# Attention of a hybrid encoder layer: filling projections in side-by-side 64-row products, and the first value products of a pair two key blocks at a time

## The reference

```
gates = sigmoid(gate_logit + gate_b);  g_A, g_B = split(gates)
m = g_A * (y_A @ w_up_gdn) + g_B * (y_B @ w_up_fox)
x = x + m @ w_out;  out = rmsnorm(x)
```

## Time and profile before

| | us |
|---|---|
| median of 3 runs | 946.38 (946.35 to 946.46) |
| the profiled execution itself | 946.32 |
| its span, first to last instruction | 944.5 |
| TensorE busy | 924.9 (98%) |
| VectorE busy | 610.3 (65%) |
| ScalarE busy | 473.1 (50%) |
| granted TensorE clock, mean | 0.999 |

### The profile page before, as it was taken

The page is one execution under the profiler, slowest core; times in us unless marked ns, Lnnn a source line. Parts: engine busy times, 40 slices in busy tenths (PEclk is TensorE's granted clock), DMA queues, the critical chain, the costliest instruction groups (busy, mean ns, idle before and its releaser), DMA issues.

```text
span 944.5 us, 15969 instructions
## 1 busy us (share of the span) xinstructions
PE 924.9 (98%) x6404; PEld 702.3 (74%) x6404; DVE 610.3 (65%) x983; ACT 473.1 (50%) x846; POOL 19.9 (2%) x29
## 2 busy tenths in 40 slices
PE   5999999999999999999999999999999999999997
PEld 5778787888888876676766666666667888888886
DVE  6487668799999934464496786767863433246252
ACT  7555654632866625532756547556554442334132
POOL 1000002020000000000000000000000000000000
PEclk9999999999999999999999999999999999999999
DMA  7111351249323393322553325234125323123162
GB/s 249 47 49 45 98 177 48 69 145 229 96 90 106 107 272 87 102 75 90 139 182 98 105 101 168 102 101 123 34 69 178 113 66 90 55 112 112 41 192 79
DMA packets 114704, 104.87 MB, mean 111 GB/s; under 512 B 33152, under 2 KB 94720, under 8 KB 114248
## 3 DMA queue, kind: packets, MB, share of 16 engines
q1 hardware_dynamic: 103256, 81.05, 30.4%
q10 hardware_dynamic: 10224, 18.62, 5.3%
q0 software_dynamic: 1152, 4.19, 1.4%
HBM read 76.84 MB, written 27.00 MB: 110 GB/s over the span
## 4 chain that ended last, share of the span: by engine, by line
PE 45%; DVE 3%; ACT 1%; DMA 1%; issue 1%; SPq 0%; DVEq 0%; ACTq 0%
PE pj L2287 6%; PE pj L2289 5%; PE pj L2288 5%; PE pc L2420 4%; PE pa L2386 3%; PE pa L2355 1%; PE pj L2298 1%; PE pj L2299 1%; PE pj L2300 1%; PE pj L2558 1%; PE pj L2556 1%; PE pj L2557 1%; PE pb L2446 1%; PE pb L2435 1%; PE pb L2557 1%; PE pb L2556 1%
## 5 line engine op out<-in xcount | busy, mean ns | idle before, releaser
L145 PE MATMUL pj<-h_hi,w_hi 128*128 128x512 f32 x504 | 203.6, 404 | 0.5 <-DVE w_lo L133 0.5
L146 PE MATMUL pj<-h_lo,w_hi 128*128 128x512 f32 x504 | 196.9, 391 | 0.0
L147 PE MATMUL pj<-h_hi,w_lo 128*128 128x512 f32 x504 | 196.5, 390 | 0.0
L145 PEld LDWEIGHTS pj<-h_hi,w_hi 128*128 128x128 f32 x504 | 94.5, 188 | 23.9 <-issue 1.1
L147 PEld LDWEIGHTS pj<-h_hi,w_lo 128*128 128x128 f32 x504 | 94.6, 188 | 20.4
L146 PEld LDWEIGHTS pj<-h_lo,w_hi 128*128 128x128 f32 x504 | 94.7, 188 | 17.9 <-issue 0.2
L2287 PE MATMUL pj<-h_hi,w_hi 128*128 128x512 f32 x248 | 101.3, 408 | 0.3 <-PEq L323 0.3
L2289 PE MATMUL pj<-h_hi,w_lo 128*128 128x512 f32 x248 | 96.8, 390 | 0.0
L2288 PE MATMUL pj<-h_lo,w_hi 128*128 128x512 f32 x248 | 96.7, 390 | 0.0
L2287 PEld LDWEIGHTS pj<-h_hi,w_hi 128*128 128x128 f32 x248 | 46.5, 188 | 19.5 <-issue 10.1
L598 ACT ACTIVATE xc<-pj 128x512 f32<-128x512 f32 x39 | 23.3, 597 | 72.2 <-PE pj L147 71.6
(11 more groups left out here) (372 smaller groups left out, 1867.9 us busy)
## 6 DMA issues: line engine op xcount, KB each, us to landing
w_raw<-in_w_in SPq DMA_DIRECT2D x48, 512.0 KB, 4.4
fox_scratch<-xc ACTq DMA_DIRECT2D x39, 256.0 KB, 2.8
qkv<-in_x SPq DMA_DIRECT2D x8, 512.0 KB, 6.4
fa<-rows_scratch POOLq DMA_DIRECT2D x8, 512.0 KB, 4.9
rv<-fr_scratch SPq DMA_DIRECT2D x16, 256.0 KB, 4.0
ma<-m_scratch SPq DMA_DIRECT2D x8, 512.0 KB, 3.9
rv<-in_w_out SPq DMA_DIRECT2D x8, 512.0 KB, 3.6
w_raw<-in_x SPq DMA_DIRECT2D x8, 512.0 KB, 4.4
```

What stands on the lines that cost most here:

```text
L145: nc.tensor.matmul(o, w_hi[:, slot, k], h_hi[:, k, cols], start=(k == 0), stop=False)
L146: nc.tensor.matmul(o, w_hi[:, slot, k], h_lo[:, k, cols], start=False, stop=False)
L147: last = nc.tensor.matmul(o, w_lo[:, slot, k], h_hi[:, k, cols], start=False, stop=(k == KT - 1))
```

## The change

Fills of tiles 1 to 7 (except one gate half) become groups of 4 k-tiles. A group multiplies the upper 64 rows of a weight with one token half and the lower 64 rows with the other half, side by side, into both halves of `pj`; a second phase swaps the halves, so that after both phases each half has all 128 rows. The number of products in a row is the same: 12 pairs stand in place of 12 whole products. A gate tile takes four groups, an up tile two. Gate and up of a tile now use the same two halves of `pj`, one after the other: an up group waits for both exponentials of the gate, the next gate for both `gated` of the tile. There are 10 groups in a pair, at steps 0, 0, 1, 2, 3, 4, 6, 8, 10, 12.

`exp_a`, `plus`, `sigmoid` and `gated` of both halves follow each other at the same step; there is a second `gate` and `mst` buffer. `gated` moves up in VectorE's steps. `values` of slots 0 and 1 are both issued in slot 2, those of 2 and 3 both ahead of slot 4's `key_scores`. The side buffer for up tile 1 goes; tile 1 is loaded where tile 2 was, its low part is made in step 0 of the first pair.

The schedule:

```diff
+        GROUPS = 10
+        GROUP_STEP = (0, 0, 1, 2, 3, 4, 6, 8, 10, 12)
+        GATE_END = [None, 1] + [7 + 6 * t for t in range(KT - 2)]
+        UP_END = [None, 3] + [9 + 6 * t for t in range(KT - 2)]
...
+        def step_of(group):
+            return -1 if group is None else PER * (group // GROUPS) + GROUP_STEP[group % GROUPS]
```

SyncE:

```diff
                 load_up(0)
-                load_up(1)
                 norm_rows(0)
                 load_raw(2)
                 sp.wait_ge(f_normed, 2)
                 load_v(0)
                 load_fox(fz, 3, 0, fz_loaded)
-                load_up(2)
+                load_up(1)
...
-                        load_up(t + 3)
+                        load_up(t + 2)
```

ScalarE:

```diff
                 def split_up_hi(tile):
+                    act.wait_ge(up_loaded, 32 * tile + 32)
+                    if 1 <= tile <= KT:
+                        act.wait_ge(up_done, 2 * tile)
...
                 def gate_exp(v, psum, dst):
-                    act.wait_ge(pj_done, 2 * N3 + v + 1)
+                    act.wait_ge(pj_done, 2 * N3 + (2 * (v // 2) + 2 if 4 <= v < 2 * KT else v + 1))
...
-                split_up_hi(1)
...
                 exp_a(2)
+                split_up_hi(1)
                 store_m(1)
```

VectorE, `gated`:

```diff
-                    dve.wait_ge(up_done, v + 1)
+                    dve.wait_ge(up_done, 2 * (v // 2) + 2 if v >= 2 else v + 1)
```

VectorE, its loop over the steps:

```diff
                     if s == 0 and p:
                         add_weights(p - 1, SLOTS - 1)
+                        gated_steps(g)
...
                         row_max(p, 0)
                         if p == 0:
-                            gated(1, gate_b1, mst_b1)
+                            gated(1)
+                            split_up_lo(1)
                         row_max(p, 1)
                         row_max(p, 2)
                         row_max(p, 3)
                         low_part(p, 1)
-                        gated_steps(g)
                         spread_max(p, 0)
                         plus_steps(g)
                         gate_steps(g)
                     elif v < 4:
                         if v < 2:
                             row_max(p, 4 + 2 * v)
+                        if v > 1:
+                            add_weights(p, v - 1)
+                        gated_steps(g)
                         if v < 3:
                             plus_steps(g)
-                        if v > 1:
-                            add_weights(p, v - 1)
                         row_max(p, 5 + 2 * v)
```

TensorE, the fills:

```diff
+                def both_halves(w, src, k, phase, first, last, done_sem, turns):
+                    for m, (w_part, s_part) in enumerate(((w[0], src[0]), (w[0], src[1]), (w[1], src[0]))):
+                        for r in range(2):
+                            half = r ^ phase
+                            ins = nc.tensor.matmul(pj[:, half], w_part[half_rows(r)], s_part[half_rows(r), k, half_cols(half)],
+                                                   start=(first and m == 0), stop=(last and m == 2))
...
+                def gate_group(tile, c):
+                    slot = (N3 + tile) % 2
+                    if c == 0:
+                        pe.wait_ge(w_ready, N3 + tile + 1)
+                        pe.wait_ge(up_free, 2 * tile)
+                    phase = c // 2
+                    if c == 2:
+                        pe.wait_ge(phase_done, 4 * tile - 4)
+                    for k in range(4 * (c % 2), 4 * (c % 2) + 4):
+                        both_halves((w_hi[:, slot, k], w_lo[:, slot, k]), (h_hi, h_lo), k, phase,
+                                    phase == 0 and k == 0, phase == 1 and k == KT - 1, pj_done, phase == 0 and k == KT - 1)
...
+                def up_group(tile, phase):
+                    if phase == 0:
+                        pe.wait_ge(up_ready, tile + 1)
+                        pe.wait_ge(pj_free, 2 * N3 + 2 * tile + 4)
...
+                    if n < 2:
+                        for k in range(4 * n, 4 * n + 4):
+                            gate_product(3, k)
```

TensorE, the pair's loop:

```diff
-                    fill(3)
+                    fill()
                     max_scores(p, 2)
                     turn_values(p, 0)
                     max_scores(p, 3)
-                    fill(5)
+                    fill()
...
                         if v == 0:
                             turn_values(p, 1)
-                        else:
-                            values(p, v - 1)
+                        if v == 2:
+                            values(p, 0)
+                            values(p, 1)
...
-                        fill(4)
+                        fill()
                     turn_max(p, 1)
                     for v in range(4, SLOTS, 2):
                         if v == 4:
+                            values(p, 2)
                             values(p, 3)
```

More of the change, by code:

```diff
@@ L1302, in program @@
         rbc, rbc_k = rv[:, 0], rv[:, 1]
-        gate_b1, mst_b1 = fa[:, 5, 0:HALF], fa[:, 6, 0:HALF]
+        gate_of, mst_of = (gate[:, :], gate_r[:, :]), (mst[:, :], mst_r[:, :])
+        up_hi = lambda tile: (up_hi_b if tile > KT and tile % 2 else up_hi_a)[:, :, :]
+        up_lo = lambda tile: (up_lo_b if tile > KT and tile % 2 else up_lo_a)[:, :, :]
         v_tok = rv[:, 1].rearrange("p (t d) -> p t d", d=P)
@@ L1701, in exp_a @@
                 def exp_a(v):
-                    act.wait_ge(up_free, 1 if v == 2 else v)
-                    gate_exp(v, pj[:, 0], gate[:, :])
+                    if v >= 2:
+                        act.wait_ge(up_free, v - 1 if v < 4 else 2 * (v // 2))
+                    gate_exp(v, pj[:, v % 2], gate_of[v % 2])
                 def store_m(v):
@@ L2065, in _ @@
                 split_w_lo(1)
-                plus(0, gate[:, :])
+                plus(0, gate_of[0])
                 for k in range(PAIRS):
@@ L2070, in _ @@
                 split_up_lo(0)
-                plus(1, gate_b1)
-                split_up_lo(1)
+                plus(1, gate_of[1])
                 normalise(0, 0)
                 normalise(0, 1)
-                gated(0, gate[:, :], mst[:, :])
+                gated(0)
                 low_part(0, 0)
@@ L2082, in gate_steps @@
                     for t in ups_split(g):
-                        split_up_lo(t + 2)
+                        split_up_lo(t + 1)
                 def plus_steps(g):
                     for u in gates_through(g - 1):
-                        if u >= 2:
-                            plus(u, gate[:, :])
+                        plus(u, gate_of[u % 2])
                 def gated_steps(g):
                     for u in units_through(g - 1):
-                        if u >= 2:
-                            gated(u, gate[:, :], mst[:, :])
+                        gated(u)
                 for g in range(STEPS + TAIL):
@@ new lines, in up_group @@
+                def up_group(tile, phase):
+                    if phase == 0:
+                        pe.wait_ge(up_ready, tile + 1)
+                        pe.wait_ge(pj_free, 2 * N3 + 2 * tile + 4)
+                    else:
+                        pe.wait_ge(phase_done, 4 * tile - 2)
+                    for k in range(PAIRS):
+                        both_halves((up_hi(tile)[:, k], up_lo(tile)[:, k]), (ya_hi, ya_lo), k, phase,
+                                    phase == 0 and k == 0, phase == 1 and k == PAIRS - 1, up_done, phase == 0 and k == PAIRS - 1)
@@ new lines, in fill @@
+                def fill():
+                    n = done[0]
+                    done[0] += 1
+                    if n < 2:
+                        for k in range(4 * n, 4 * n + 4):
+                            gate_product(3, k)
+                    elif n < 4:
+                        up_group(1, n - 2)
+                    else:
+                        tile, c = 2 + (n - 4) // 6, (n - 4) % 6
+                        if c < 4:
+                            gate_group(tile, c)
+                        else:
+                            up_group(tile, c - 4)
@@ L2317, in fill @@
[L2317 to L2319 removed]
+                        gate_product(2 * KT + v, k)
                 def head_sums(p):
```

143 lines of the change are left out of this document (63 added, 80 removed).

## The result

The changed kernel takes 963.81 us (median of 4 runs, 961.28 to 965.37) against 946.42 for the kernel before on the same chip: ratio 1.0171, 95% interval 1.0153 to 1.0189. It is slower, as forecast, but by 17.4 us and not 5.6, and outside the range. The profiled execution took 965.37 us, with a span of 963.6 (944.5 before). Behind the last `weight_sums` both kernels take the same 226.3 us to the end of the span, and they reach the first pair within 0.7 us of each other; all of the difference lies in the four pairs. The four runs order by the clock that TensorE was granted, as a mean of the span: 961.28 us at 0.996, 963.40 at 0.994, 964.21 at 0.992, 965.37 at 0.991.

The account below looks back on a forecast made before the run. The prediction took TensorE's dense row of products (busy 98% of the span) as the bound. Waits of 19.2 us less 13.4 saved gave 5.8 more than 946.3: 952 us, main range 948.5 to 956, wider range 942 to 958.

Parts of the forecast that it names:

- the clock: Rival: TensorE idle in (a) drops to half rate, 2 to 4 us lost, 955 us; chance 0.10.
- old late starts: TensorE's present waits in the stage, mostly tied to the old order, counted as all gone: 3.2 us.
- the saving: In the four pairs, 51 fewer changes of array shape (10.2 us) plus present waits gone (3.2): 13.4 us.
- (e): Third pair, steps 0 and 1: `plus` behind `spread_max`, sigmoids behind both; the group needing `up_free` waits 2.1 us.
- (f): First pair's step 9, two sigmoids ahead of an exponential, and the tail's first gate: 0.3 us each, 0.6.
- (a): First pair, step 0: `split_up_lo(1)`, waiting for its load, delays `row_max(1)` and what follows: 5.1 us.
- (d): Steps 4 to 6, second and third pair: TensorE's group waits for VectorE's lengthened chain, 1.6 us each, 3.2.
- (b): Step 0 of pairs two to four: VectorE's chain through `spread_max` ends after TensorE needs it, 2.8 us together.
- (c): Slots 2 and 3: later paired values delay `add_weights(1)` and the chain freeing `max_scores(11)`'s bank, 5.4 us together.
- the waits don't add up: Rival: 10 us of waits go, 942 us, or 935 if only (a) stays; chance 0.17.
- no change: Rival: only half of the waits come, 946 to 948 us; chance 0.13.
- The products don't overlap: Rival: paired 64-row products in different halves of `pj` run one after the other, 105 us added; chance under 0.01.

Follow-up runs that it names:

- e2: Changed kernel with ScalarE's `split_w_hi(3)` moved from step 1 to the end of step 3: 960.13 us.
- e4: Changed kernel with 15 useless products put into each of the first pair's two long TensorE waits, no wait removed: 962.62 us.
- e7: Kernel before with only the pairing of value products added, fills still on the whole array: 947.58 us.
- e12: e9 with ScalarE's two sigmoids and `split_w_hi(7)` in the third pair's slot 4 moved behind the exponentials of slot 5: 942.96 us.
- e13: e12 with the value products of slots 0 to 3 issued one block at a time: 942.60 us.
- e9: e3 with further VectorE and ScalarE instructions moved in the first three pairs, and VectorE's order in step 0 and slot 2 changed: 946.61 us.
- e10: e9 with whole-array fills in place of side-by-side ones: 952.04 us.
- e3: Changed kernel with `split_up_lo(1)` moved behind `spread_max` on VectorE and `split_w_hi(3)` moved to step 3 on ScalarE: 955.89 us.

## Why the prediction failed

The prediction had the sign and the mechanism, 5.8 us of net loss out of waits, and 0.70 on slower. By the two traces the stage grew by 19.8 us (262.63 against 242.87). The 14 us between the two are a missed wait (3.4), the clock (6.5) and a saving that fell short (5.9), less 1.9 by which the other waits came out lower (the 3.2 us of old late starts counted as gone). Three steps failed: the list of places left one out, the sum put the clock at nothing, and the saving was sized too high. By the prediction's steps:

- **First failed step: the list of places in "What it adds", 3.4 us.** It said "I go through the places where less time lies between release and need than the work takes", and it names ScalarE's order for its sigmoids alone, in (e) and (f); the splits of the gate weights (`split_w_hi`) stand nowhere in it. `split_w_hi(3)` went from behind the exponentials of slot 1 to in front of them, and waits there for a load that SyncE can issue only at 495.56, when `split_w_lo(2)` has read the buffer. This is a wait of 3.4 us, the largest along with (a), and it is in no term (e2: 3.0 to 3.7 us with what follows it). The exponential of slot 5 in the third pair, behind four sigmoid passes and a split, is another, 1.1 us. The diff shows both as changed step numbers alone, `tiles_through` and `gates_through`; what stands around the call had to be read at each of these steps.
- **Second failed step: the clock, nothing in the sum, a rival at 0.10 and 2 to 4 us for one place.** It cost at least 6.5 us, in three places. I set it against one long stretch, and judged that "hardly longer than the one behind the last product". The third pair shows that no single long stretch is needed: behind waits of 0.85 and 1.25 us the clock fell at 621.35, within the second of them, and stayed down to 628.18. The Trainium skill ("TensorE: Matmul & The Clock Gate", "A second HAM failure mode: psum-queue depth-cycling") tells of a kernel in which small pauses between groups of products make the clock swing; this trace agrees, at 0.50 in that stretch. But the same two waits, 0.84 and 1.26 us, left it at 1.00 in the profiles of e2 and e4, so they bring it down in some executions only.
- **Third failed step: the saving, 13.4 us.** I took 51 x 0.20 = 10.2 us as time won. The count was right within one (147 to 95 in the traces), but with the 6.5 us of half clock taken off, TensorE is busy for only 4.3 us less in the changed kernel: 5.9 are missing. About 2 of them are the pairing, whose 13 changes, between value and score products, are worth 0.3 (e7) and 0.2 us (e12 against e13) together. About 2 are the price of the other 39: TensorE is busy for 5.9 us less in e12 than in e7, 0.15 each, and 0.18 each in e9 against e10; the 0.20 was read where 64-row and whole-array products meet and taken for all. The last 1.9 are gone in e12, which has the same products and changes of shape with fewer waits; why the waits lengthen the busy time is not shown. The 3.2 us of old late starts can't be told apart from the new waits: of 2.2 us idle before, the waits on record name VectorE's `mpart` for 1.1, which stays in the changed kernel (3.4) and in e12 (2.2), and so doesn't look tied to the old order of values and exponentials. TensorE is idle for 5.3 us in e12.
- **(a), 5.1 us.** Right in kind and near in size: `row_max(1)` is 3.3 us late (forecast 4.0), TensorE waits 3.4, and the third fill 1.2 for the exponential of unit 3 (forecast 0.7). There too a weight split was left out of the chain: `split_w_hi(2)` stands ahead of that exponential, 491.08 to 492.03. Wrong in one point: `max_scores(3)` reuses a bank that `row_max(1)` reads, so the wait falls ahead of the second fill and not behind it; that fill then ran at half clock. `turn_max` is at 488.40, forecast "near 487".
- **(d) and (e), 3.2 and 2.1 us.** Right. From `key_scores(4)` to the fill it is 3.53 and 3.54 us in the second and third pair against 1.95 in the others, 1.6 each; the third pair's slot 0 is 2.1 longer than before. Moving the named instructions in e9 took away all of (d); of (e) a wait of 0.8 us for `gated` is left.
- **(b) and (c), 2.8 and 5.4 us.** Too high: 0.3 a pair in (b), and in (c) 1.1 in the first and fourth pair, 0.5 in the second, none in the third: 3.6 for the two, of 8.2. Each was a difference between two chains, and TensorE came to them later than I had put it, because the changes brought less.
- **(f), 0.6 us.** Right in kind for the first pair, too low, and one place short: the exponential of slot 9, behind two sigmoids and a split, costs 0.6 in the first and 0.6 in the fourth pair (forecast 0.3 and none).
- **A slip in the rivals.** With (a) alone left, the sum is 946.3 + 5.1 - 13.4 = 938, not 935. Nothing hangs on it.

Idle time was forecast at some 15 us and is 19.7: without the missed 3.4 the sum of waits was right within 2 us, by errors of both signs. The rivals "the waits don't add up" and "no change" are out by the time, and by 19.7 us of idle time. "The products don't overlap" is out by the 0.227 us between pairs.

Open: which of the short waits brings the half clock down in slot 0 and in the third pair. In e3 it fell at other places than in the changed kernel, in e2 and e4 not at all in the third pair with the same waits, and the changed kernel itself spreads over 4.1 us between runs, e12 over 1.2.

## What to carry to other kernels

When the work that fills an engine is regrouped, list every instruction whose step number changes, on every queue, and write beside each what now stands behind it; one load-fed split ahead of an exponential cost about as much here as 20 changes of array shape won. In this dense product stream (98% busy) a wait could cost twice, the second time by the clock behind it; count it wherever idle time gathers, not only where it is long. And time taken out of the bound engine is won only if those that feed it are ahead: here the same fills lost 17 us or won 4, by where VectorE's and ScalarE's small instructions stood.

## What the runs showed of the hardware

The half clock cost 1.24 to 2.5 us for each stretch inside a fill, and it came behind gathered waits of 0.85 and 1.25 us as well as behind one of 3.43; behind the same two short waits it did not come in e2 and e4. Products issued into the idle time kept it at 1.0 (e4). A change between 64-row and whole-array fills is worth 0.15 to 0.18 us of TensorE's busy time and 0.14 us of the kernel's here; the 13 changes between value and score products that the pairing takes out are worth 0.2 to 0.3 us together. The Trainium skill ("TensorEngine Tiling (Array Packing)", "Tiling Modes") says that a change of mode drains the engine; the cost of the fills' changes agrees with that, the near nothing of the pairing's doesn't show it. From the issue of `up_raw` to ScalarE's copy of it 6.3 us pass in the changed kernel, 6.7 in e2 and 7.1 in e4; with the issue itself, which moves by up to 0.8, the length of wait (a) changes by over 1 us.
